# Four buffers for squares, wide residual and closing products, and a reordered head pipeline in a two-block fp32 kernel

## What is computed

```
block 1:  mod = silu(c) @ w_ada + b_ada
          h   = rmsnorm(x, g0) * (1 + sc_m) + sh_m
          q,k,v,g,u,gates = split(h @ w_in)
          ret = group_norm(retention(rope(q), rope(k), v))      # 8 heads, value width 256
          y_s5 = glu(gelu(s5_ssm(u)) @ w_s5_glu)
          x   = x + gt_m * rmsnorm((sig(gate_r)*((silu(g)*ret) @ w_ret_out)
                                    + sig(gate_s)*y_s5) @ w_out, g1)
          h   = rmsnorm(x, g2) * (1 + sc_f) + sh_f
          x   = x + gt_f * rmsnorm((silu(h@a) * (h@b)) @ w_ffn_out, g3)
block 2:  h   = rmsnorm(x);  proj = h @ w_in                     # attention, gated linear
          x   = x + (sum of 3 gated branches) @ w_out            # attention, short convolution
          x   = x + (silu(rmsnorm(x)@gate) * (rmsnorm(x)@up)) @ down
return rmsnorm(x) * final_norm_w
```

## Time and profile before

| | |
|---|---|
| median of 3 runs | 3454.16 us (3452.05 to 3454.35) |
| profiled execution | 3456.49 us |
| its span in the trace | 3454.6 us |
| PE busy | 3298.0 us, 95% of the span |
| DVE busy | 2389.5 us, 69% |
| ACT busy | 1494.9 us, 43% |
| one product at full clock | about 5.85 us |

### The profile page before, as it was taken

How to read it: one execution, slowest core, us unless ns; L and a number is a source line. 1 busy time by engine, 2 the same in 40 slices (tenths; PEclk the granted TensorE clock), 3 DMA queues, 4 the chain that set the end, 5 groups by cost and what they waited for, 6 DMA issues and landing times.

```text
span 3454.6 us, 53480 instructions
## 1 busy us (share of the span) xinstructions
PE 3298.0 (95%) x20912; PEld 2990.6 (87%) x20912; DVE 2389.5 (69%) x2467; ACT 1494.9 (43%) x1538; POOL 445.8 (13%) x309
## 2 busy tenths in 40 slices
PE   1799999999989999999989999999999999999998
PEld 0799999999978888888868888888888888888887
DVE  8799987787676666655676667657767766666554
ACT  1455555544444344433354344344344444434332
POOL 2065556720100000000000000000002100000000
PEclk7899999999999999999999999999999999999999
DMA  9665554568745555567734444555555555555554
GB/s 399 269 235 219 217 206 173 187 246 302 300 151 184 194 186 190 190 233 258 266 111 167 171 159 175 191 182 190 193 183 198 185 190 187 193 185 190 190 190 146
DMA packets 111026, 706.34 MB, mean 204 GB/s; under 512 B 13376, under 2 KB 24256, under 8 KB 30672
## 3 DMA queue, kind: packets, MB, share of 16 engines
q1 hardware_dynamic: 100416, 693.86, 54.8%
q10 hardware_dynamic: 10512, 11.11, 1.0%
HBM read 702.83 MB, written 2.10 MB: 204 GB/s over the span
## 4 chain that ended last, share of the span: by engine, by line
PE 82%; DVE 8%; issue 4%; ACT 3%; POOL 2%; DMA 2%; DVEq 0%; ACTq 0%; POOLq 0%; SPq 0%
PE acc L523 44%; PE acc L524 23%; PE acc L520 4%; PE acc L521 4%; PE acc L522 4%; DVE ring_lo L1307 2%; ACT ring_hi L859 1%; DMA ring_raw<-w_ada 1%; DVE ring_raw L1329 1%; POOL s_w L1985 1%; PE p_norm L569 1%; POOL s_x L1987 0%; DVE aside_y L1329 0%; PE p_y L587 0%; POOL s_x L1984 0%
## 5 line engine op out<-in xcount | busy, mean ns | idle before, releaser
L1307 DVE TENSOR_TENSOR ring_lo<-ring_raw,ring_hi 128x2048 fp32r<-128x2048 f32 (+1 forms) x576 | 1312.4, 2280 | 571.8 <-ACT ring_hi L859 570.3
L523 PE MATMUL acc<-h_split,ring_hi 128*128 128x512 f32 x4736 | 1655.5, 392 | 9.2 <-DVE h_split L1369 4.5
L524 PE MATMUL acc<-h_split,ring_lo 128*128 128x256 f32 x4736 | 1337.5, 282 | 0.0
L859 ACT ACTIVATE ring_hi<-ring_raw 128x2048 fp32r<-128x2048 f32 (+1 forms) x576 | 1070.8, 1862 | 414.4 <-DMA ring_raw<-w_down 152.0
L523 PEld LDWEIGHTS acc<-h_split,ring_hi 128*128 128x128 f32 x4736 | 891.7, 188 | 197.3 <-issue 9.7
L524 PEld LDWEIGHTS acc<-h_split,ring_lo 128*128 128x128 f32 x4736 | 897.7, 190 | 0.4
L523 PE MATMUL acc<-ffn_split,ring_hi 128*128 128x512 f32 x1408 | 488.2, 390 | 0.0
L520 PE MATMUL acc<-h_split,ring_hi 128*128 128x256 f32 x1408 | 403.7, 287 | 82.9 <-DVE h_split L1369 69.8
L1926 POOL TENSOR_TENSOR sq_sum<-sq_sum,tile 128x256 f32<-128x256 f32 x60 | 76.6, 1277 | 2568.9 <-ACT tile L885 2568.9
L524 PE MATMUL acc<-ffn_split,ring_lo 128*128 128x256 f32 x1408 | 397.1, 282 | 0.0
L521 PE MATMUL acc<-h_split,ring_hi 128*128 128x256 f32 x1408 | 396.3, 281 | 0.0
(11 more groups left out here) (342 smaller groups left out, 3814.2 us busy)
## 6 DMA issues: line engine op xcount, KB each, us to landing
ring_raw<-w_ff SPq DMA_DIRECT2D x88, 1024.0 KB, 4.8
ring_raw<-w_down SPq DMA_DIRECT2D x64, 1024.0 KB, 4.8
ring_raw<-w_ffb SPq DMA_DIRECT2D x56, 1024.0 KB, 4.8
ring_raw<-w_heads SPq DMA_DIRECT2D x48, 1024.0 KB, 4.8
ring_raw<-w_mix SPq DMA_DIRECT2D x48, 1024.0 KB, 4.8
ring_raw<-w_ada SPq DMA_DIRECT2D x32, 1024.0 KB, 7.4
ring_raw<-w_ret SPq DMA_DIRECT2D x32, 1024.0 KB, 4.8
ring_raw<-w_glu SPq DMA_DIRECT2D x32, 1024.0 KB, 4.9
```

The costliest lines, as they stand in the source:

```text
L523: mm(dst[:], hi[s][:, t, :], moving[:, k, :], start=start, stop=False, skip_group_check=True)
L524: return mm(dst[:, T:], lo[s][:, t, :], moving[:, k, 0:T], start=False, stop=stop, skip_group_check=True)
L859: run(hi[s][:, 0:n, :], raw[s][:, 0:n, :], COPY).then_inc(hi_done, 1)
L1307: tt(lo[s][:, 0:n, :], raw[s][:, 0:n, :], hi[s][:, 0:n, :], SUB).then_inc(lo_done, 1)
```

## The change

- `tile` has four buffers for squares instead of two, and ScalarE waits for the use of the square four before.
- Behind out1 the gain is applied by ScalarE as it takes the sum out; VectorE multiplies by rstd and adds in wide instructions over 2, 2, 4, 4, 2, 1 and 1 columns (`SUM_GROUPS`). Behind down1 `residual` keeps one multiplication a column and adds in the same groups.
- At the end ScalarE applies the gain column by column during down2's squares, VectorE multiplies by rstd in groups of 1, 1, 2, 4, 4, 2 and 2 columns (`OUT_GROUPS`), and SP stores each group.
- In heads, ScalarE's `ret_step(3)` moves behind the `evac` of the value tile, VectorE's `ret_before(3)` behind `s5_turned_back`, and `ret_before(4)` behind `ahead`.
- In the opening of ret, TensorE multiplies the last head's values behind product 0 and turns it back behind product 2; ScalarE's and VectorE's steps for it move to earlier products.
- In attention the transposes stand one product later (r = 2), and the product with the values and what follows move to r = 0 of the next head; in the opening of gla likewise.

```diff
         rstd = sb(ctx, "rstd", [P, T])
-        tile = [sb(ctx, f"tile{i}", [P, T]) for i in range(2)]
+        tile = [sb(ctx, f"tile{i}", [P, T]) for i in range(4)]
         eps = sb(ctx, "eps", [P, 4])
...
             (1, 0), (0, 8), (1, 1), (0, 11), (1, 3), (1, 4), (1, 2), (1, 6), (1, 7), (1, 5), (1, 9), (1, 10), (1, 8), (1, 11)]
+
+        SUM_GROUPS = [(0, 2), (2, 2), (4, 4), (8, 4), (12, 2), (14, 1), (15, 1)]
+        OUT_GROUPS = [(0, 1), (1, 1), (2, 2), (4, 4), (8, 4), (12, 2), (14, 2)]
...
                             sp.dma_start(aside[name][k][:], src).then_inc(aside_in[k], 16)
-            for kt in range(0, KT, 2):
-                sp.wait_ge(out_ready, kt + 2)
-                sp.dma_start(out[kt:kt + 2].rearrange("k p t -> p k t"), x[:, kt:kt + 2, :]).then_inc(out_sent, 16)
-            sp.wait_ge(out_sent, 16 * KT // 2)
+            for j, (k, n) in enumerate(OUT_GROUPS):
+                sp.wait_ge(out_ready, j + 1)
+                sp.dma_start(out[k:k + n].rearrange("k p t -> p k t"), x[:, k:k + n, :]).then_inc(out_sent, 16)
+            sp.wait_ge(out_sent, 16 * len(OUT_GROUPS))
...
                     pe.wait_ge(sq_done, KT * stage + kt + 1)
-                    mm(p_norm[:, 0:T], ones[:], tile[kt % 2][:], start=kt == 0, stop=kt == KT - 1).then_inc(sq_used, 1)
+                    mm(p_norm[:, 0:T], ones[:], tile[kt % 4][:], start=kt == 0, stop=kt == KT - 1).then_inc(sq_used, 1)
...
                 pe.wait_ge(sq_done, KT * (stage + 1))
-                mm(p_norm[:, 0:T], ones[:], tile[1][:], start=False, stop=True).then_inc(sq_used, 1)
+                mm(p_norm[:, 0:T], ones[:], tile[3][:], start=False, stop=True).then_inc(sq_used, 1)
...
                     product(p, g, m, [(m, 0, 16, ret_flat if m >= 4 else h, 0)], last)
-                    if opening(g) and m in (1, 3):
-                        steps[3 * m // 2 + 1](ph["heads"].iters, 0, HEADS)
+                    if opening(g) and m in (0, 2):
+                        steps[3 * m // 2 + 2](ph["heads"].iters, 0, HEADS)
                     s5_steps("ret", g, m)
...
-            steps = [att_scores, att_turn, att_values]
             p = ph["att"]
...
                     i, r = divmod(m, 3)
+                    n = 4 * g + i
                     if not (opening(g) and m < 2):
...
                     if not (opening(g) and i == 0):
-                        steps[r](g, i, 4 * g + i, (i + 1) % 2)
+                        if r == 0:
+                            if not (opening(g) and i == 1):
+                                att_values(g, i, n - 1, i % 2)
+                            att_scores(g, i, n, (i + 1) % 2)
+                        elif r == 2:
+                            att_turn(g, i, n, (i + 1) % 2)
                     elif r == 0:
...
                         gate_up()
-            att_rest = steps
+
+            def att_rest(r):
+                if r == 0:
+                    att_values(ph["att"].iters, 0, HEADS - 1, 0)
+                    att_scores(ph["att"].iters, 0, HEADS, 1)
+                elif r == 2:
+                    att_turn(ph["att"].iters, 0, HEADS, 1)
+                elif r == 3:
+                    att_values(ph["att"].iters, 0, HEADS, 1)
...
                 n = kt + (16 * stage)
-                if not isinstance(n, int) or n >= 2:
-                    act.wait_ge(sq_used, n - 1)
+                if not isinstance(n, int) or n >= 4:
+                    act.wait_ge(sq_used, n - 3)
                 run(tile[par][:], src, ACT.Square).then_inc(sq_done, 1)
...
                             act.wait_ge(R["masked"], n)
-                        if r in (3, 4):
+                        if r == 4:
                             ret_step(r, g, i, n)
                     evac(p, g, m, m, (qk[:, 0, :], qk[:, 1, :], v_t[:, 0, :], v_t[:, 1, :], g_t[:, 0, :], g_t[:, 1, :])[r])
-                    if r == 0 and not (opening(g) and i == 0):
+                    if r in (0, 3) and not (opening(g) and i == 0):
                         ret_step(r, g, i, n)
...
                 for m in range(8):
-                    if opening(g) and m == 4:
+                    ahead(p, g, m)
+                    if opening(g) and m == 3:
                         ret_step(5, ph["heads"].iters, 0, HEADS)
-                    ahead(p, g, m)
                     s5_steps("ret", g, m, early=True, end=end)
-                    if opening(g) and m in (2, 3):
-                        ret_step(m + 1, ph["heads"].iters, 0, HEADS)
+                    if opening(g) and m == 2:
+                        ret_step(4, ph["heads"].iters, 0, HEADS)
                     if m < 4:
                         evac(p, g, m, m, m_ret[:, 4 * g + m, :], tanh=True)
+                        if opening(g) and m == 1:
+                            ret_step(3, ph["heads"].iters, 0, HEADS)
                     else:
...
                                 product_done(p, g, m)
-                                square_of(stage, acc[o % 2][:, 0:T], d, o % 2)
-                                evac(p, g, o, m, y[:, d, :])
+                                square_of(stage, acc[o % 2][:, 0:T], d, o)
+                                run(y[:, d, :], acc[o % 2][:, 0:T], ACT.Identity, scale=gain[:, 1, one(d)]).then_inc(evac_done, 1)
                             else:
...
                                     act.wait_ge(y_done, d + (16 * updates + 1))
-                                square_of(stage, y[:, d, :], d, o % 2)
+                                square_of(stage, y[:, d, :], d, o)
+                                if updates == 3:
+                                    run(x[:, d, :], x[:, d, :], ACT.Identity, scale=gains[:, 6, one(d)]).then_inc(x_scaled, 1)
                                 if updates == 2:
...
                     ins.then_inc(A["exp"], 1)
-                elif r == 1:
+                elif r == 2:
                     act.wait_ge(A["p_turned"], n)
                     run(ex_t[:], p_z[:, 0:T + P], COPY).then_inc(A["p_t"], 1)
-                else:
-                    act.wait_ge(A["summed"], n)
-                    run(o_att[:, 4 * g + i - 1, 0:T], p_o[:, 0:T], COPY).then_inc(A["hi"], 1)
...
                 inverse_std(stds)
-                with dve.Fori(0, KT // 4) as q:
-                    own.enter(4, q)
-                    marks = []
-                    for b in range(4):
-                        k = 4 * q + b
-                        marks.append(own.mark(stt(y[:, k, :], y[:, k, :], gain[:, i, one(k)], rstd[:], MUL, MUL)))
-                    for b in range(4):
-                        k = 4 * q + b
-                        dve.wait_ge(dve_own, marks[b])
-                        tt(x[:, k, :], x[:, k, :], y[:, k, :], ADD).then_inc(y_done, 1)
-                    own.leave(KT // 4)
+                for j, (k0, n) in enumerate(SUM_GROUPS):
+                    for k in range(k0, k0 + n):
+                        ins = stt(y[:, k, :], y[:, k, :], gain[:, i, k:k + 1], rstd[:], MUL, MUL)
+                    ins.then_inc(y_times, 1)
+                    dve.wait_ge(y_times, len(SUM_GROUPS) + j + 1)
+                    at = slice(k0, k0 + n)
+                    tt(x[:, at, :], x[:, at, :], y[:, at, :], ADD).then_inc(y_done, n)
...
                     n = 2 * g + i
-                    if prev[i] and r == 4:
-                        ret_before(r, g, i, n)
                     ahead(p, g, m)
-                    if prev[i] and r != 4:
+                    if prev[i] and r != 3:
                         ret_before(r, g, i, n)
                     s5_turned_back("heads", g, m)
+                    if prev[i] and r == 3:
+                        ret_before(r, g, i, n)
                     if r == 2:
...
                 for m in range(8):
-                    if opening(g) and m == 3:
+                    ahead(p, g, m)
+                    if opening(g) and m == 2:
                         ret_before(4, *last_head)
-                    elif opening(g) and m == 4:
+                    elif opening(g) and m == 3:
                         ret_out(HEADS)
+                    s5_turned_back("ret", g, m)
+                    if opening(g) and m == 1:
+                        ret_before(3, *last_head)
+                    elif opening(g) and m == 3:
                         ret_done(HEADS - 1, HEADS)
-                    ahead(p, g, m)
-                    s5_turned_back("ret", g, m)
-                    if opening(g) and m == 2:
-                        ret_before(3, *last_head)
                     if m >= 4:
...
             dve.wait_ge(x_in, 2 * 16)
-            residual(y1, 1, 2)
+            inverse_std(2)
+            dve.wait_ge(evac_done, ph["out1"].out_count(ph["out1"].iters - 1, 3))
+            for j, (k, n) in enumerate(SUM_GROUPS):
+                at = slice(k, k + n)
+                tt(y1[:, at, :], y1[:, at, :], rstd[:].unsqueeze(1).to_broadcast([P, n, T]), MUL).then_inc(y_times, 1)
+                dve.wait_ge(y_times, j + 1)
```

(19 more changed lines are left out.)

24 lines of the change are left out of this document (16 added, 8 removed).

## The result

The changed kernel takes 3467.18 us in the median of 5 runs (3466.08 to 3471.67), the kernel before 3454.35 beside it (3452.05 to 3457.66). The ratio is 1.0038, with an interval of 1.0025 to 1.0050: slower by about 13 us. The profiled execution is the median one, 3467.18 us, with a span of 3465.4 us, 10.8 more than the span before.

What follows compares the result with a forecast made beforehand. The prediction took the loop of VectorE, ScalarE and GpSimd to bound heads, TensorE elsewhere save at norms. Terms summed to +8.25 us on the profiled 3456.5, giving 3464.7; less 2.3 for that execution, 3462.4, range 3447 to 3471.

Steps and rivals of the forecast that it cites:

- likeliest case: Whole kernel: the forecast's own case, range 3455 to 3470 us; chance 0.60.
- Rival C: Heads: TensorE is the bound and its waits were the cost; 3426 us, or 3436 if ret's opening pays part; chance 0.14.
- rival B: Heads: the loop's other holes take up the added idle time, only the opening of ret pays; 3454 us; chance 0.17.
- Second heads: Heads, i = 1, four times: reciprocal and shift behind the split delay the GELU; +0.84 us each, +3.4 in all.
- First heads: Heads, i = 0, three times: later statistics delay ring_hi and VectorE's split, part comes back; +1.77 us each, +5.3 in all.
- Rival D: Heads: GpSimd's multiplications stay slow, so first heads cost 15.9 us instead of 5.3; 3473 us; chance 0.09.
- The signs: Rows of the later profile named in advance as showing the prediction right or wrong, such as a heads period of 88.7 us.
- the wait of about 9 us ahead of L635: Opening of ret: a wait of about 9 us expected there, named as a sign that the prediction is right.
- Opening of ret: Turn back ahead of product 3 instead of behind it: product 4 starts 7.3 us later, bounds +4 to +9.
- Behind out1 and down1: Norms behind both: wide instructions and four square buffers bring the reciprocal earlier, −2.4 us behind out1, −1.35 behind down1.
- Attention: One more product between softmax and transposes shortens two TensorE waits by 1.8 and 2.2 us; −4.0, bounds −2 to −5.5.
- the end: Last stores: begin 0.45 us earlier, but the DMA engines are full; 0, ±0.5 us.

Runs made afterwards that it cites:

- evac_first: both_old with ScalarE taking v_t out ahead of the root, as the changed kernel does, VectorE's order as before; 3448.81 us, 0.9980 of the kernel before.
- short_asides: evac_first with each of VectorE's five w_ada sums in an iteration of heads over 256 instead of 2048 columns; 3431.28 us, 0.9932 of the kernel before.
- heads_old: The changed kernel with its three moves inside heads undone; 3458.68 us, 1.0011 of the kernel before.
- stats_first: evac_first with the statistics one step earlier, ahead of VectorE's split at that product; 3438.29 us, 0.9949 of the kernel before.
- scale_late: evac_first with only the reciprocal and shift moved behind VectorE's split; 3454.44 us, 0.9993 of the kernel before.
- stats_late: evac_first with only the statistics moved behind the turning back; 3450.78 us, 0.9985 of the kernel before.
- both_old: The changed kernel with the old order in heads and the old opening of ret; 3450.25 us, 0.9979 of the kernel before.
- stats_first_ret: stats_first with the last head's statistics ahead of the split at product 2 in the old opening of ret; 3437.45 us, 0.9946 of the kernel before.

## Why the prediction was right

The forecast was 3462.4 in a range of 3447 to 3471; measured 3467.2. Its likeliest case held, and its size was low by 4.8 us. The bound and the direction were right for the reason given; the sizes of single terms were right in part by luck, as is said under each, and two of the signs named in advance did not come.

**What bounds heads.** The claim that heads goes by the loop of VectorE, ScalarE and GpSimd, and that TensorE's 11.0 us at v_t are its slack, is shown from both sides: evac_first takes the 11.0 us away and gains 2; short_asides takes work from VectorE alone and gains 18. Rival C, 3426, fell with that, and rival B, with no cost in heads, with heads_old. ScalarE's part in the loop is shown by stats_first. GpSimd's is only read from the rows (VectorE waits for it 0.7 us an iteration); no experiment changed its work. The page "Perfetto Trace Analysis" of the Trainium skill ("Identifying the Most-Contended Engine") tells to optimize the most-contended engine first, the one of highest occupancy, where TensorE is to be judged by the share of its peak rate and by its weight loads, not by its busy matmuls. Here that is TensorE by its weight loads too, over the span (87%, VectorE 69%) and, narrowly, in heads (80.0 of 86.1 us against 78.2). The runs show that the loop that bounds heads is made of other engines, none of them the busiest.

**Second heads, +0.84 each.** The row shows +0.87. scale_late puts 5.6 us on this move, against 4 to 5 expected of it alone.

**First heads, +1.77 each.** The period between roots of first heads is 88.66 us (272.96 to 361.62) against 86.12, +2.54, where 0.84 + 1.77 = 2.61 was forecast. The sum is right; that it came from the late statistics is only half right, as stats_late shows, and that is luck. The terms of the prediction add up to a turning back at 368.5 (361.4, 2.28, 0.34, 2.2 and 2.3), and it had 369.3; the 0.8 between has no row, and the changed kernel has a wait of 0.94 us for ring_hi there, which comes from the late reciprocal. One reading was wrong: the split of 2.28 us in the earlier trace rows was not "without company". It lies from 358.47 to 360.75, and GpSimd's 3.42 us from 358.49 to 361.91, so nearly all of it beside that split and not beside the aside. What came back was still as forecast (3.39 to 2.29, 2.81 to 2.29). Rival D fell: the aside takes 2.29 us. Its price was off as well: with the aside at 3.39 and the next split at 2.81 the same terms give 370.2, or 371.0 with the 0.8, so 2.7 to 3.5 us a head and not 5.3. A time near 3467 would thus not have excluded D; the row of the aside does. "SBUF — State Buffer", "Who interferes with whom", in the Trainium skill has VectorE and GpSimd lock each other out at a shared pair of ports; the rows agree, in both directions (3.39 to 2.29 for the one, 3.42 to 1.29 for the other).

**The signs.** The period of 88.65 us, no wait at v_t, the rows of out1 and L723 and the aside of 2.29 us came as named. The root's wait in first heads did not fall from 9.03 us to some 3: it is 8.00, and it fell to 3.2 (from 11.4) only in second heads. The evacuation took the place ahead of the root, but the statistics came later as well. VectorE's wait for ring_hi in first heads is 4.28 us (2.59 with the late statistics alone) where about 3 was named. And the wait of about 9 us ahead of L635 is 5.85, with 3.72 for the scores two products earlier.

**Opening of ret, +7.3.** This is the term that was mis-sized. It was worked out for the start of product 4, and there it is +10.6. The prediction called the wait for masked scores one "that the one to come swallows". TensorE does not lose it twice, but product 1 ends later by it, at 523.07, and ScalarE, which takes products out in order, comes to the root only behind that evacuation and a table load of 1.28 us: the root ends at 525.1, where the chain of the prediction, moved by the 10.3 us by which this product 0 starts later, had 524.1. The split that follows takes 2.99 us beside GpSimd and not 2.25. One of GpSimd's instructions was running when it started, and ended at 530.99. Together 1.8 us at o_t (534.5 against 532.7). Another 1.5 us come behind it. The prediction let product 3 start 0.8 us behind o_t, but between them stand the turn back and the S5 matmuls of L600, which take 1.92 us behind the wait at a granted clock of 0.50 (1.02 in the kernel before, where they are L597, at 513.03): product 3 starts at 536.78, 2.3 us behind o_t. That is the 3.3 us missing. Product 4 then takes 7.2 us where it took 8.5 with the turn back just ahead of it (granted clock 1.00 against 0.85), and that gain of 1.3 was not forecast either; so by product 5 the term stands at +9.3.

**Behind out1 and down1.** −2.35 and −1.35 to −2.4 and −1.35. The first repeats itself in all kernels with four buffers (−2.1 to −2.4). The second does not (−0.5 to −1.4 in the same code), so that it was met to the hundredth is luck. The wide multiplication with a broadcast operand takes 1.22 us over 1024 elements, no more than the plain addition it was priced by.

**Attention, −3.8 to −4.0; the end, −0.1 to 0.** No experiment undid them alone. The same code of attention gives −2.9 to −4.5 us in the thirteen kernels that have it. both_old bears the gains out in the sum: −7.3 by the ratio against −7.75.

**What stays open.** The terms with their measured sizes add to +10.8 with the 1.0 at the start, the 1.6 given back ahead of out1 and the 0.5 behind it, which is the difference of the spans; the forecast had +8.25, so 2.5 us of the 4.8 are terms. The medians differ by 12.8: the profiled execution of the kernel before lay 2.3 us above its median and that of the changed kernel on it, so the other 2.3 us are what runs of one kernel differ by. Why the same move did nothing in the opening of ret (stats_first_ret) is open.
